# No warm-up products behind the first scores of three attention calls

## The reference

```
logits = einsum('bqhcd,bkhcd->bhcqk', q, ka) * 64**-0.5          # half A: 4 heads, 2 components of 64
p      = softmax(where(causal, logits, -inf))
attn   = p[:, :, 0] - lam * p[:, :, 1]                            # the components are mixed
out_a  = einsum('bhqk,bkhe->bqhe', attn, va)                      # values of width 128

logits = einsum('bqhd,bqkhd->bhqk', q, k_g) * 64**-0.5            # half B: 8 heads of 64,
p      = softmax(where(valid, logits, -inf))                      # each row of 512 attends to the 128 keys
out_b  = einsum('bhqk,bqkhd->bqhd', p, v_g)                       # that an index score picked
```

```
o = softmax(q k^T / 8 + bias[distance]) v
```

## Time and profile before

| | us |
|---|---|
| median of three runs | 3377.85 |
| lowest and highest | 3376.58, 3378.3 |
| profiled execution, its own time | 3373.97 |
| span in its profile | 3372.3 |
| TensorE matmul busy (PE) | 2904.1 (86%) |
| VectorE busy | 862.1 (26%) |
| ScalarE busy | 425.8 (13%) |
| mean granted TensorE clock | 0.943 |

### The profile page before, as it was taken

One profiled execution on the slowest core, in us unless ns is written; L12 is line 12 of the kernel. 1 busy time (PEld: TensorE's weight loads), 2 busy tenths in 40 slices (PEclk: granted clock), 3 DMA queues, 4 the chain that ended last, 5 costly groups with the idle time before them and its releaser, 6 DMA issues. The chain is left out here.

```text
span 3372.3 us, 25197 instructions
## 1 busy us (share of the span) xinstructions
PE 2904.1 (86%) x9791; PEld 1334.5 (40%) x9791; DVE 862.1 (26%) x2038; ACT 425.8 (13%) x879; POOL 55.5 (2%) x149
## 2 busy tenths in 40 slices
PE   9793789999999999999997957397598888888887
PEld 4341445444444444444443424264332333333232
DVE  3546633100001313420003035543411111111112
ACT  2102423100001013111000011240000000000000
POOL 0000000000000000100000010000000000000000
PEclk9896889999999999999998977698699999999999
DMA  7111001222222212752221210101299999999997
GB/s 278 50 38 62 1 1 63 75 75 75 75 75 78 75 50 73 250 187 75 84 79 38 75 51 0 50 1 51 99 427 429 429 428 428 429 429 429 429 428 321
DMA packets 107003, 572.36 MB, mean 170 GB/s; under 512 B 11517, under 2 KB 12277, under 8 KB 82341
## 3 DMA queue, kind: packets, MB, share of 16 engines
q1 hardware_dynamic: 99104, 540.74, 39.7%
q0 software_dynamic: 6768, 29.43, 2.5%
q10 hardware_dynamic: 1045, 1.04, 0.1%
HBM read 569.05 MB, written 6.32 MB: 171 GB/s over the span
## 5 line engine op out<-in xcount | busy, mean ns | idle before, releaser
L2271 PE MATMUL banks<-ring,ex_x 128*64 128x512 f32 x2048 | 466.6, 598 | 76.8 <-DMA ring<-in_w_up 43.5
L203 PE MATMUL banks<-hT,ring 128*128 128x512 f32 x1088 | 469.2, 594 | 6.8 <-PEq L296 5.1
L203 PEld LDWEIGHTS banks<-hT,ring 128*128 128x128 f32 x1088 | 207.1, 191 | 267.1 <-issue 267.1
L2271 PEld LDWEIGHTS banks<-ring,ex_x 128*64 128x64 f32 x2048 | 136.5, 136 | 392.5 <-issue 239.5
L206 PE MATMUL banks<-ring,hT 128*128 128x512 f32 x640 | 277.1, 595 | 5.5 <-ACT e_KTb L1336 3.6
L2271 PE MATMUL banks<-ring,mod 128*64 128x512 f32 x1024 | 227.5, 595 | 31.0 <-DMA ring<-in_w_down 23.8
L322 PE MATMUL banks<-ring,m_u 128*128 128x512 f32 x512 | 220.3, 592 | 1.6 <-PEq L176 1.6
L206 PE MATMUL banks<-ring,m_u 128*128 128x512 f32 x512 | 220.0, 592 | 1.6 <-PEq L176 1.6
L206 PEld LDWEIGHTS banks<-ring,hT 128*128 128x128 f32 x640 | 121.9, 191 | 160.1 <-issue 155.6
L206 PEld LDWEIGHTS banks<-ring,m_u 128*128 128x128 f32 x512 | 97.2, 190 | 124.4 <-issue 124.4
L322 PEld LDWEIGHTS banks<-ring,m_u 128*128 128x128 f32 x512 | 97.0, 190 | 123.4 <-issue 123.4
(11 more groups left out here) (573 smaller groups left out, 2551.3 us busy)
## 6 DMA issues: line engine op xcount, KB each, us to landing
ring<-in_w_up SPq DMA_DIRECT2D x80, 2048.0 KB, 15.8
ring<-in_w_down SPq DMA_DIRECT2D x80, 2048.0 KB, 15.8
ring<-in_w_gate SPq DMA_DIRECT2D x64, 2048.0 KB, 15.5
ada_rows<-in_w_ada POOLq DMA_DIRECT2D x32, 768.0 KB, 4.7
ring<-in_w_in_e SPq DMA_DIRECT2D x5, 2048.0 KB, 8.9
ring<-in_w_in SPq DMA_DIRECT2D x5, 2048.0 KB, 7.9
ring<-in_wkv_x SPq DMA_DIRECT2D x4, 2048.0 KB, 25.4
ring<-in_w_in_o SPq DMA_DIRECT2D x4, 2048.0 KB, 7.9
```

Of the source, the lines that this page charges most:

```text
L203: mm = nc.tensor.matmul(o, w[:, k, a:z], src[:, ka, 0:ntok], start=(ka == 0), stop=(ka == kc * kgroups - 1))
L2271: mm = nc.tensor.matmul(g.psum[64 * e:64 * e + 64, bank, :], lhs(q * half + k)[:, 64 * e:64 * e + 64], w[:, e, k, :], start=first, stop=last)
```

## The change

The argument `warm=5` is left out of the three calls, so that `warm_up` issues nothing.

```diff
@@ even_mixer
-            attend(g, "e_attA", units, 2, P, lambda un, ps, r: nc.vector.tensor_copy(un["out"], ps), 64 ** -0.5, warm=5)
+            attend(g, "e_attA", units, 2, P, lambda un, ps, r: nc.vector.tensor_copy(un["out"], ps), 64 ** -0.5)
@@ even_mixer
             attend(g, "e_attB", units, 1, 64,
-                   lambda un, ps, r: nc.vector.tensor_scalar(un["out"], ps, r, None, ALU.mult), 64 ** -0.5, warm=5)
+                   lambda un, ps, r: nc.vector.tensor_scalar(un["out"], ps, r, None, ALU.mult), 64 ** -0.5)
@@ second_block
         attend(g, "s_att", units, 1, 64,
-               lambda un, ps, r: nc.vector.tensor_scalar(un["out"], ps, r, None, ALU.mult), 0.125, warm=5)
+               lambda un, ps, r: nc.vector.tensor_scalar(un["out"], ps, r, None, ALU.mult), 0.125)
```

## The result

The changed kernel took 3465.76 us in the median of six executions (3398.56 to 3469.23), the kernel before 3376.12. Repeated in a second set of runs it took 3465.4 us, and there the ratio to the kernel before is 1.0275, with a 95% interval of 1.0258 to 1.0292. Forecast was 3366.2. The first set holds two more executions, of 3467.62 and 3397.7 us.

The account below looks back on a forecast made before the run. No transfer bounds the changed stretches; unread TensorE warm-up products sit on the path. Savings of 4.3 + 4.3 + 3.9 less 0.9 for the clock give 11.6 us, so 3377.85 becomes 3366.2 us, range 3361.5 to 3372.

Parts of the forecast that it names:

- What the warm-ups cost: At the heads of the three attention calls: warm-ups delay the first transposes by 4.3, 5.8 and 3.6 us.
- A: Differential attention call (L1438): scores of unit 1 start earlier without the warm-up, saving 4.3 us at unchanged clock.
- S: Dilated attention call (L2452): full clock throughout, saving 3.9 us, between 3.6 and 4.5.
- B: Sparse attention call (L1446): 5.8 us gained at its head, 1.5 lost to the clock, saving 4.3, between 2.8 and 4.9.
- The clock in A: Differential attention: an earlier clock fall or further slow stretch, taken as 0.4 of one, costs 0.9 us.
- more than two slow stretches: Differential attention: a test that the forecast is wrong if more than two lower-clock stretches stand within the call.
- the clock in B: Sparse attention: real work raises the clock as the warm-up did; slow stretch 2.7 to 6.1 us, loss 1.5 us.
- The size per slow microsecond: Price of lower clock, from the differential attention's cadence: 0.33 us lost per slow us, bound 0.5.
- Rival three: Sparse attention never wakes the clock without its warm-up: 30 us more there, net 18 slower, 3396 us; chance 0.03.
- Rival four: Last third, bound by the weight stream: the dilated attention's 3.9 us saving vanishes, 3370 us; chance 0.04.

Follow-up runs that it names:

- the run that begins slow: Kernel before with ten VectorE memsets ahead of the sparse attention (TensorE idle 23.7 us) and that call's warm-up left out: 3437.05 us.

## Why the prediction was wrong

**What the warm-ups cost: right.** They were on the path. A's took 4.3 us at its head, as forecast. The first transpose of S comes 2.9 us after the first scores where it came 6.6 (3.6 forecast), that of B 1.6 where it came 7.7 (5.8 forecast). The run without A's warm-up alone gained 4.6 us.

**The clock in A: the term had the wrong sign.** The forecast took 0.9 us back there; A is 6.8 us shorter, 2.5 more than its head. I had read one slow stretch in A before (353.3 to 360.1), but it has three, two of them in its second half, and the last (from 387.4) covers its end. The changed kernel has three as well, at nearly the same mean clock (0.86, 0.85 before), but none at its end: from VectorE's last peak to B's first scores pass 7.4 us, 9.0 before, which is 1.6 of the 2.5. So "more than two slow stretches" could not tell a failed forecast: the kernel before has more than two. All this is small beside what follows.

**The step that failed is the clock in B: "all of B's work at the lower level keeps TensorE full just as the warm-up did".** It did keep TensorE full (79.75 of 80 us), and the clock stayed at 0.50. Being busy and raising the clock are not the same thing here. I priced the slow stretch of B at 1.5 us and gave it at most 6.1 us of length; it lasted from 392 to past B's end at 483 (the projection behind it, from 503 on, is at 1.00). B's stretch grew by 29.8 us, and that is net of the warm-up: from the first to the last peak B takes 89.7 us, and 55.0 without a warm-up at full clock, so the lower level cost 34.7. The size per slow microsecond was too low as well: 0.33 from A, but 0.40 in B (91.9 us in the run that begins slow, 55.0 at full clock) and 0.47 in S. The evidence I took for it was A's stretch that ended at 360.1. But A's two components lie in rows 0 to 63 and 64 to 127 and their score records run side by side: four of 512 columns take 1.13 us at 343.64 above, and in S two of them take 1.12. A was no model for B. That its pairs of scores are what raises the clock in A is argued from these rows, not tested; that B's scores do not is shown. The `64*128` of L564 stood in the trace all the time.

**S: the same step, by a road that I had excluded.** "The stretch 2176.5:2262 is at full clock throughout, the call begins in it, and its work is dense" was read in the kernel before, with the warm-up in that stretch. With the warm-up the clock stayed up or, where it fell, came back within it (2181.63 above); without it the head is loose (TensorE idle for 1.3 us ahead of the first scores and 0.6 before the first transpose in the changed kernel), and the clock fell there and stayed low in nine of twelve executions of the changed kernel, by their times, and in four of four with S's warm-up alone left out. I forecast 3.9 us of saving and found 62.8 of loss. A full clock before a call is no proof that the call keeps it, when what held it is being removed.

**Rival three was the right mechanism** ("B's own products, two records per score and waits between them, do not" raise it), at a chance of 0.03. It had 30 us of loss in B, where 34.7 came, and 3396 us in all; the three executions near 3398, by their times with S still fast, lie beside it. That closeness is in part luck: net of the warm-up it had 25.7 us of loss in B, where the table has 29.8, and 3.4 of gain in A, where it has 6.8. It lacked the cause, and it lacked S. The argument against it, that B at full clock never fell in 398:459, is true and beside the point: B stayed at whichever level it had (1.00 in 394:450 without a warm-up, 0.50 in 400:480).

**A slip without effect.** Rival four has the DMA engines at 9 tenths from slice 29 on; the page reads 2 in the 29th and 9 from the 30th.

**Transposes, and a busy TensorE.** The clock rose again behind nothing but transposes (0.50 in 2203:2207.5, 0.98 in 2208:2211), so for these float32 transposes the row stands, and the sentence of the Trainium skill on them (page "TensorE: Matmul & The Clock Gate", section "PE-mode transpose"), which the prediction cites, does not. The Trainium skill, page "TensorE: Matmul & The Clock Gate", section "Why this matters for your kernels", advises to keep TensorE continuously busy to reach full rate; this trace is against that rule as it stands, with TensorE busy 142.61 of 143 us at 0.50.

**What stays open.** What decides which of its two kinds an execution of S, or of B alone, will be was not found out; nothing that the kernel issues differs between them. The slow kind of the kernel without B's warm-up (3410 to 3416) lies some 15 us above the 3398 of the changed kernel, and the warm-ups of A and S explain 8 or 9 of that. And the stretch between B and S differs by some 6 us among profiles of kernels that do the same there, which was not followed.

## What to carry to other kernels

Before products that nobody reads are removed, ask what the granted clock is around them and whether the work behind them can raise it by itself; a stretch that reads 1.00 with them in it says nothing of that. Look at the rows of the operands, not at the busy share: a call whose products fill half of the array's rows may stay at the lower clock from end to end with a full TensorE. Padding the contraction with zeros to all rows can be the better cure (25 us here); look what the engine that makes the zeros holds up.

## What the runs showed of the hardware that was not expected

- At the lower level, half-row products did not raise the clock in 21 us without a gap, nor in 82 and 143 us of attention work; full-row ones did within 5 to 6 us. At full clock, operands that are half zero held it.
- Half-row scores cost time at full clock too. With full rows and the same columns, VectorE's 30 steps from the second peak to the last (which leaves out a warm-up) take 66.1 us in place of 73.9 in S, and 49.0 in place of 54.5 in B. The weight loads show where: TensorE's loader begins with the transpose's weights 0.47 us after it has finished those of the scores, not 0.76. In the rows below both brackets name ScalarE, whose exponentials end at 2234.49 and 2232.81. With full rows the loader follows them by 0.05 us, and 0.36 before the scores end; with half rows it stands 0.64 us longer and begins only 0.07 us before the scores end. The kernel before, then the one with full rows, both within S:

```profile
2235.13 0.42 PEld L574 LDWEIGHTS banks<-ident,s_att_probs 128*128 128x128 f32 x4 [0.76 <-ACT s_att_probs L653]
```

```profile
2232.86 0.56 PEld L574 LDWEIGHTS banks<-ident,s_att_probs 128*128 128x128 f32 x4 [0.47 <-ACT s_att_probs L653]
```

- The lower level costs less than a factor of two: S's 30 steps from the second peak to the last took 138.5 us against 73.9, a factor of 1.87, and B's 31 steps, without a warm-up, 91.9 against 55.0, a factor of 1.67.
- A GpSimd copy or memset of 64x2048 float32 elements, 1.8 to 1.9 us long, held VectorE's instructions beside it: one of 0.17 us took 1.76, one of 0.29 took 1.57.
